# The two heads of a pair alternate block by block in the product of probabilities and values

## The chip, the cores and the metric

The kernel runs on one core of a Trainium2 chip. The metric is the device time of one execution in microseconds, as the median of several runs. The matrix engine (PE, TensorE) multiplies; its weight loads are recorded apart from its products (PEld). VectorE (DVE), ScalarE (ACT) and GpSimd (POOL) work element by element, and SyncE (SP) issues most transfers.

## The reference, cut to what matters

One decoder layer on a sequence of 512 tokens with width 1024: an adaptive RMS norm, a mixture of three causal dilated window attentions with 16 heads of 64 per group, an output projection, a gated convolutional feed-forward layer of width 2816, and a last norm. The change touches the attention alone:

```
def dilated_mixture_attention(h, w_in, w_out):
    qkv = (h @ w_in).reshape(B, S, 3, DSW_GROUPS, DSW_HEADS, DSW_HEAD_DIM)
    for g, (window, dilation) in enumerate(((128, 1), (512, 4), (2048, 16))):
        o, lse = dilated_window_attention(qkv[:, :, 0, g], qkv[:, :, 1, g], qkv[:, :, 2, g], window, dilation)
        ...
    weights = jax.nn.softmax(jnp.stack(lses, axis=0), axis=0)
    o = jnp.sum(weights[..., None] * jnp.stack(outs, axis=0), axis=0)
    return o.reshape(B, S, D_MODEL).astype(h.dtype) @ w_out
```

In each group a query attends to a band of keys. The probabilities, weighted by the mixture, times the values give `o`. That last product, `einsum('brnhqk,brnkhe->brnqhe', p / denom, v)`, is the one whose order is changed.

## The kernel before, in words

The 16 heads are worked in 8 pairs. A pair's heads stand side by side in 128 partitions: head 0 in partitions 0 to 63, head 1 in 64 to 127. `body` (line 716) runs nine passes: pass n projects q, k and v of pair n (nine strips of 1024 x 128 weights, each in two halves of 12 products, `half_strip`, lines 604 to 606) and, between these halves, does the attention of pair n - 1. The first pass only projects. The last, for the eighth pair, only attends, and fills the room between its steps with the first products of the output projection (`begin_out`, lines 684 to 686). Each engine has its program written out by hand, in the order of the half strips h = 0 to 17; semaphores join them.

Attention of a pair has four parts j = 0 to 3, each two tiles of 128 queries with up to two blocks of 128 keys. j 0 and 1 are the first group (bank 6), j 2 and 3 the two dilated groups (bank 7).

- `make_scores` (lines 621, 628): queries times keys, contraction over 64 partitions; the two heads already alternate there, into a bank each.
- VectorE adds the mask and takes the maximum (line 1202), ScalarE exponentiates (953), VectorE mixes and scales (1218), which it counts in `scaled`.
- `turn_probs` (line 657): the matrix engine transposes the scaled probabilities, head 0 into bank 4 and head 1 into bank 5. VectorE copies bank 4 into p_t (line 1192, semaphore `turn_taken0`), ScalarE bank 5 (line 923, `turn_taken1`). p_t has four slots; part j with head hd uses slot (2j + hd) mod 4.
- `weigh_values` (line 676): values (128 keys x 64 columns, the weights) times p_t (128 keys x 128 queries, moving), into `o_acc[side]`. Head 0's 64 columns go to PSUM partitions 0 to 63, head 1's to 64 to 127, of the same bank. j = 0 has three blocks per head, the others four.
- When the last part is through (`pv_done`), ScalarE copies bank 6 to o_a (966), VectorE adds bank 7 (1294), ScalarE rounds to oh (970), VectorE takes the rest as ol (1299), and `o_summed` lets the next pair's product begin.

The parts are placed by tables: transposes of part 0, 1, 2, 3 after half strip 12, 14, 15, 16, the product of part 0, 1, 2, 3 after half strip 14, 15, 16, 17, ahead of the transposes at the same place.

Of the kernel before, what the change touches and what calls it, by code (L numbers as in the profile page):

```python
# [25 lines left out]
P = 128  # L26
# [4 lines left out]
H, E = 16, 64  # L31
# [18 lines left out]
PT_RING = 4  # L50
# [25 lines left out]
def decoder_layer(nc, x, c, w_ada, b_ada, norm_mix, norm_ffn, attn_w_in, attn_w_out,  # L76
# [11 lines left out]
    with ctx:  # L88
# [3 lines left out]
        def sem(name):  # L92
            return ctx.enter_context(nc.semaphore(name))
# [28 lines left out]
        v_n = tensor(scope_a, "v_n", [P, 2, GROUPS, NT, P])  # L122
        v_t = tensor(scope_a, "v_t", [P, 2, T])
        probs = tensor(scope_a, "probs", [P, 2, 2, NT, HALF])
        p_t = tensor(scope_a, "p_t", [P, PT_RING, T])
# [46 lines left out]
        proj, score, turn, o_acc = banks[0:2], banks[2:4], banks[4:6], banks[6:8]  # L172
# [30 lines left out]
        turn_taken = [sem("turn_taken0"), sem("turn_taken1")]  # L203
        scored, masked, nmax_done, exp_done = sem("scored"), sem("masked"), sem("nmax_done"), sem("exp_done")
        swapped, mix_dve, mix_act = sem("swapped"), sem("mix_dve"), sem("mix_act")
        scaled, pv_done = sem("scaled"), sem("pv_done")
# [15 lines left out]
        def turns_before(n):  # L222

            return 0 if isinstance(n, int) and n == 0 else 6 * n - 4
# [7 lines left out]
        PV_AT = {14: 0, 15: 1, 16: 2, 17: 3}  # L232
# [307 lines left out]
        def _(pe):  # L540
# [4 lines left out]
            for t in range(KT):  # L545
                if t >= 4:
                    pe.wait_ge(start_taken, t - 3)
                for i in range(NT):
                    last = nc.tensor.transpose(banks[t % 4][:, P * i:P * (i + 1)], x_nat[:, i, P * t:P * (t + 1)], ident[:])
# [9 lines left out]
            for t in range(KT):  # L559
                pe.wait_ge(start_taken, KT + 2 + t - 3 if t >= 4 else KT - 3 + t)  # L560
                for i in range(NT):
                    last = nc.tensor.transpose(banks[t % 4][:, P * i:P * (i + 1)], xr_nat[:, i, P * t:P * (t + 1)], ident[:])
# [95 lines left out]
                                               probs[:, hd, j // 2, b, P * part:P * (part + 1)], ident[:])  # L658
                last.then_inc(turned[k], 1)

            def weigh_values(n, par, u, before):
                hd, j, k = u % 2, u // 2, u % 2
                e = slice(E * hd, E * (hd + 1))
                pe.wait_ge(turn_taken[k], turns_before(n) + before + j + 1)
                if u == 0:
                    pe.wait_ge(o_summed, n)
                side = j // 2
                blocks = p_blocks(j)
                for i, (b, part) in enumerate(blocks):
                    if side == 0:  # L670
                        values = v_n[:, par, 0, b - 1 + part, e]
                    else:
                        values = v_n[:, par, 1 + part, b, e]
                    first = i == 0 or blocks[i - 1][0] != b
                    final = i == len(blocks) - 1 or blocks[i + 1][0] != b
                    last = nc.tensor.matmul(o_acc[side][e, P * b:P * (b + 1)], values, p_t[:, u % PT_RING, P * i:P * (i + 1)],  # L676
                                            start=first, stop=final)
                last.then_inc(pv_done, 1)

            def out_tiles(o, tiles, tokens=slice(0, T)):  # L680
# [35 lines left out]
            def body(n, par, project, attend):  # L716
                before = 2 if project else 0
                filled = 0
                for h in range(2 * RING if is_first(n) else 0, HALVES):
                    s = h // 2  # L720
                    if project:
                        g = STRIPS * n + s
                        if h % 2 == 0:
                            pe.wait_ge(l_ready, g + 1)
                            if not (is_first(n) and s == RING):
                                pe.wait_ge(strip_taken, g - 1)
                        last = half_strip(qkv_bank(n, par, s), qkv_slot(n, s), h % 2, hh, hl)
                        if h % 2 == 1:
                            last.then_inc(strip_done, 1)
                        turn_v_at = TURN_V_FIRST if is_first(n) else TURN_V_AT  # L730
                        if h in turn_v_at:
                            turn_values(n, par, turn_v_at[h])
                        if h == (ADA_FIRST if is_first(n) else ADA_AT):
                            sum_ada(n)
                    if attend:
                        if h in SCORE_AT:
                            make_scores(n, 1 - par, SCORE_AT[h])
                        if h in PV_AT:
                            for u in (2 * PV_AT[h], 2 * PV_AT[h] + 1):
                                weigh_values(n, 1 - par, u, before)  # L740
                        if h in TURN_P_AT:
                            for u in (2 * TURN_P_AT[h], 2 * TURN_P_AT[h] + 1):
                                turn_probs(n, u, before)
                    if attend and not project and h in FILL_AT:
                        begin_out(fill_steps[filled:filled + FILL_AT[h]])
                        filled += FILL_AT[h]
# [21 lines left out]
            for hf in range(2):  # L768
                tokens = slice(HALF * hf, HALF * (hf + 1))
                for t in range(KT):  # L770
# [5 lines left out]
                    for j in range(2):  # L776
                        nc.tensor.matmul(banks[j][:, tokens], wl_first[:, j, t], fh[:, t, tokens], start=(t == 0), stop=False)
                        nc.tensor.matmul(banks[j][:, tokens], wh_first[:, j, t], fh[:, t, tokens], start=False, stop=False)
                        last = nc.tensor.matmul(banks[j][:, tokens], wh_first[:, j, t], fl[:, t, tokens],
                                                start=False, stop=(t == KT - 1))  # L780
# [49 lines left out]
            for o in range(KT):  # L830
                for k in (FT - 2, FT - 1):
# [3 lines left out]
                    last = nc.tensor.matmul(y_bank(o)[:], wh[:, slot, o], act_l[:, k], start=False, stop=(k == FT - 1))  # L835
                last.then_inc(y_done, 1)
                for m in BACK_AT.get(o, ()):

                    pe.wait_ge(x2_done, 4 if m < 4 else KT if m < 6 else KT + 1)
                    for q in range(4):  # L840
                        last = nc.tensor.transpose(y_bank(m)[:, P * q:P * (q + 1)],
                                                   xT[:, 4 * (m // 4) + q, P * (m % 4):P * (m % 4 + 1)], ident[:])
# [4 lines left out]
        def _(act):  # L847
# [77 lines left out]
            def body(n, par, project, attend):  # L925
                before = 2 if project else 0
                for h in range(HALVES):
                    s = h // 2
                    if project:
                        if split_at(n, h) is not None:  # L930
                            split_qkv(n, split_at(n, h))
                        if h % 2 == 1:
                            act.wait_ge(strip_done, STRIPS * n + s + 1)
                            kind, g = strip_of(s)

                            if is_first(n) and s == 2:
                                act.wait_ge(turned[0], 1)
                            dst = {"v": v_t[:, (par + g) % 2], "q": q_t[:, par, g], "k": k_t[:, par, g]}[kind]
                            src, dst = in_order(g, kind, qkv_bank(n, par, s)[:], dst)
                            nc.scalar.activation(dst, src, ACT.Copy).then_inc(strip_taken, 1)  # L940
                        if (TURN_V_FIRST if is_first(n) else TURN_V_AT).get(h) == 1:
                            take_turn(n, 0, v_n[:, par, 1].rearrange("p b e -> p (b e)"))
                    if attend and not project and h == 0:
                        split_out(split_h, 3, h_ready, wh)
                    if attend:
                        if h in SCORE_AT:
                            d = SCORE_AT[h]
                            act.wait_ge(nmax_done, 4 * (n - 1) + d + 1)
                            side = d // 2
                            for b in (2 * (d % 2), 2 * (d % 2) + 1):  # L950
                                for hd in range(2):
                                    tile = probs[:, hd, side, b, (P if d == 0 and b == 0 else 0):HALF]
                                    last = nc.scalar.activation(tile, tile, ACT.Exp, bias=nmax[:, side, b, hd:hd + 1],  # L953
                                                                scale=SCORE_SCALE, accum_out=stat[:, side, b, 1, hd:hd + 1])
                            last.then_inc(exp_done, 1)
                        if h == 8:
                            act.wait_ge(mix_dve, MIX_STEPS * (n - 1) + 3)
                            nc.scalar.activation(mix[:, 3:5], mix[:, 1:3], ACT.Exp, scale=SCORE_SCALE).then_inc(mix_act, 1)
                        if h in TURN_P_AT:
                            u = 2 * TURN_P_AT[h] + 1  # L960
                            take_turn(n, before + u // 2, p_t[:, u % PT_RING])
                    if is_last(n) and h == HALVES - 2:
                        split_out(split_h, 2, h_ready, wh)
                if attend:
                    act.wait_ge(pv_done, 8 * n)
                    nc.scalar.activation(o_a[:].rearrange("p (b j r) -> p b j r", b=NT, r=4),
                                         o_acc[0][:].rearrange("p (b r j) -> p b j r", b=NT, r=4),
                                         ACT.Copy).then_inc(oa_copied, 1)
                    act.wait_ge(o_summed, n + 1)
                    nc.scalar.activation(oh[:, bass.ds(n - 1, 1)].rearrange("p a n -> p (a n)"), o_sum[:],  # L970
                                         ACT.Copy).then_inc(oh_done, 1)
# [531 lines left out]
```

## Time and profile before

| | |
|---|---|
| median of 3 runs | 1021.26 us (1020.44 to 1022.64) |
| profiled execution, first to last instruction (its span) | 1017.7 us |
| matrix engine busy | 973.8 us, 96% |
| VectorE busy | 514.6 us, 51% |
| ScalarE busy | 403.3 us, 40% |
| product of probabilities and values (line 676), busy | 47.1 us |
| transposes of the probabilities (line 657), busy | 33.0 us |

Of the profiled execution the profile has the span alone; the runs are timed as a whole, and their median is 3.6 us more than the span. Busy time of a group is the time in which at least one of its records ran, so records that overlap aren't counted twice. The start of a matrix record is measured, its end modelled.

### The profile page before, as it was taken

To read this page: it belongs to the slowest core of one execution; us is meant where nothing else is said; L and a number is where in the kernel's file an instruction comes from. 1 tells how busy PE (TensorE), PEld (TensorE's weight loads), DVE (VectorE), ACT (ScalarE), POOL (GpSimd) and SP (SyncE) were. 2 spreads that over 40 slices of the span, in tenths; PEclk is the share of its full clock that TensorE was granted. 3 is DMA by queue.
4 is the path that set the end of the run, shared out by engine and by line. 5 is a ranking of instruction groups with operands and counts; after the bars stand their busy time and mean duration, and the time that the engine had idled before them with its cause. 6 is when DMAs were issued, how large, how long until landed. Compare 5 with 4: busy or idle time off the path is not lost.

```text
span 1017.7 us, 14215 instructions
## 1 busy us (share of the span) xinstructions
PE 973.8 (96%) x5008; PEld 784.4 (77%) x5008; DVE 514.6 (51%) x1115; ACT 403.3 (40%) x721; POOL 31.3 (3%) x43
## 2 busy tenths in 40 slices
PE   4589999999999999999999989999999999999996
PEld 3478787887877878878778779888888888888885
DVE  5863663655735646357365557644444444412214
ACT  7433443434435344353443534633333333321212
POOL 3500000000000000000000000100000000000000
PEclk9699999999999999999999999999999999999999
DMA  9746341432324314333232203333333323232212
GB/s 310 210 116 194 112 133 48 125 118 90 95 89 123 124 41 124 124 103 124 62 114 74 62 22 90 100 101 91 95 97 89 102 83 103 83 104 86 99 62 83
DMA packets 151533, 106.94 MB, mean 105 GB/s; under 512 B 3510, under 2 KB 138830, under 8 KB 151502
## 3 DMA queue, kind: packets, MB, share of 16 engines
q1 hardware_dynamic: 151296, 106.45, 34.4%
q8 instruction: 19, 0.31, 0.1%
q14 instruction: 12, 0.10, 0.0%
q10 hardware_dynamic: 206, 0.08, 0.0%
HBM read 104.42 MB, written 2.10 MB: 105 GB/s over the span
## 4 chain that ended last, share of the span: by engine, by line
PE 92%; DVE 5%; ACT 1%; issue 1%; DMA 1%; SPq 0%; DVEq 0%; POOL 0%; ACTq 0%
PE bank L604 13%; PE bank L606 13%; PE bank L605 13%; PE bank L797 8%; PE bank L798 8%; PE bank L799 8%; PE bank L676 4%; PE bank L822 4%; PE bank L821 4%; PE bank L823 4%; PE bank L657 3%; PE bank L628 2%; PE bank L621 1%; DVE acc L1093 1%; PE bank L684 1%; PE bank L686 1%
## 5 line engine op out<-in xcount | busy, mean ns | idle before, releaser
L1131 DVE TENSOR_TENSOR wl<-raw,wh 128x1024 fp32r<-128x1024 f32 x144 | 177.4, 1232 | 305.1 <-ACT wh L883 304.6
L883 ACT ACTIVATE wh<-raw 128x1024 fp32r<-128x1024 f32 x144 | 152.2, 1059 | 200.8 <-PE bank L799 112.9
L604 PE MATMUL bank<-hh,wl 128*128 128x512 f32 x552 | 227.0, 411 | 0.0
L606 PE MATMUL bank<-hl,wh 128*128 128x512 f32 x552 | 218.7, 396 | 0.0
L605 PE MATMUL bank<-hh,wh 128*128 128x512 f32 x552 | 218.3, 395 | 0.0
L799 PE MATMUL bank<-fl,wh 128*128 128x512 f32 x336 | 133.0, 396 | 0.0
L798 PE MATMUL bank<-fh,wh 128*128 128x512 f32 x336 | 133.0, 396 | 0.0
L797 PE MATMUL bank<-fh,wl 128*128 128x512 f32 x336 | 133.0, 396 | 0.0
L604 PEld LDWEIGHTS bank<-hh,wl 128*128 128x128 f32 x552 | 104.1, 189 | 27.8 <-issue 5.7
L606 PEld LDWEIGHTS bank<-hl,wh 128*128 128x128 f32 x552 | 103.9, 188 | 24.7
L605 PEld LDWEIGHTS bank<-hh,wh 128*128 128x128 f32 x552 | 104.1, 189 | 20.7
L953 ACT ACTIVATE probs<-probs,nmax 128x256 f32<-128x256 f32 (+1 forms) x128 | 61.9, 485 | 98.4 <-DVE nmax L1208 98.4
L797 PEld LDWEIGHTS bank<-fh,wl 128*128 128x128 f32 x336 | 63.2, 188 | 15.3
L799 PEld LDWEIGHTS bank<-fl,wh 128*128 128x128 f32 x336 | 63.2, 188 | 15.2
L798 PEld LDWEIGHTS bank<-fh,wh 128*128 128x128 f32 x336 | 63.2, 188 | 15.1
L822 PE MATMUL bank<-act_h,wh 128*128 (+1 forms) x160 | 63.4, 396 | 0.0
L823 PE MATMUL bank<-act_l,wh 128*128 (+1 forms) x160 | 63.4, 396 | 0.0
L821 PE MATMUL bank<-act_h,wl 128*128 (+1 forms) x160 | 63.3, 396 | 0.0
L1192 DVE COPY p_t<-bank 128x512 f32<-128x512 f32 x32 | 22.1, 690 | 61.7 <-PE bank L657 61.7
L923 ACT ACTIVATE p_t<-bank 128x512 f32<-128x512 f32 x32 | 19.1, 598 | 79.4 <-PE bank L657 79.4
L676 PEld LDWEIGHTS bank<-p_t,v_n 128*64 128x64 f32 x480 | 39.4, 136 | 12.0 <-issue 10.7
L676 PE MATMUL bank<-p_t,v_n 128*64 128x128 f32 x480 | 47.1, 279 | 0.3 <-DVE p_t L1192 0.3
(175 smaller groups left out, 1147.7 us busy)
## 6 DMA issues: line engine op xcount, KB each, us to landing
raw<-in_attn_w_in SPq DMA_DIRECT2D x72, 512.0 KB, 3.8
raw<-in_ffn_w_up SPq DMA_DIRECT2D x44, 512.0 KB, 3.8
ada_raw<-in_w_ada SPq DMA_DIRECT2D x16, 1024.0 KB, 5.7
raw<-in_ffn_w_down SPq DMA_DIRECT2D x22, 512.0 KB, 3.3
ada<-in_w_ada SPq DMA_DIRECT2D x16, 256.0 KB, 7.1
raw<-in_attn_w_out SPq DMA_DIRECT2D x8, 512.0 KB, 3.6
x_nat<-in_x SPq DMA_DIRECT2D x4, 512.0 KB, 5.2
x_nat<-in_w_ada SPq DMA_DIRECT2D x8, 256.0 KB, 6.3
```

Source lines behind the costliest of these rows:

```text
L604: nc.tensor.matmul(bank[:], wl[:, slot, t], xh[:, t], start=(t == 0), stop=False)
L605: nc.tensor.matmul(bank[:], wh[:, slot, t], xh[:, t], start=False, stop=False)
L606: last = nc.tensor.matmul(bank[:], wh[:, slot, t], xl[:, t], start=False, stop=(t == KT - 1))
L676: last = nc.tensor.matmul(o_acc[side][e, P * b:P * (b + 1)], values, p_t[:, u % PT_RING, P * i:P * (i + 1)], start=first, stop=final)
L797: nc.tensor.matmul(bank[:], wl[:, slot, t], fh[:, t], start=(t == 0), stop=False)
L798: nc.tensor.matmul(bank[:], wh[:, slot, t], fh[:, t], start=False, stop=False)
L799: last = nc.tensor.matmul(bank[:], wh[:, slot, t], fl[:, t], start=False, stop=(t == KT - 1))
L821: nc.tensor.matmul(y[:], wl[:, slot, o], xh, start=start, stop=False)
L822: nc.tensor.matmul(y[:], wh[:, slot, o], xh, start=False, stop=False)
L823: last = nc.tensor.matmul(y[:], wh[:, slot, o], xl, start=False, stop=False)
L883: nc.scalar.activation(dst, src, ACT.Copy).then_inc(done, 1)
L1131: nc.vector.tensor_tensor(dst, src, high.bitcast(F32), ALU.subtract).then_inc(done, 1)
```

## The change

In `weigh_values` the loop over the two heads moves inside the loop over blocks: where all blocks of head 0 stood ahead of all of head 1, block after block now comes for head 0 and then for head 1. The function is called once for a part and not once for a head, so it waits at its start for both heads' copies into p_t, and counts `pv_done` once a part (4 for a pair, where there were 8). No product is added, removed or resized, and the order within a head stays.

```diff
-            def weigh_values(n, par, u, before):
-                hd, j, k = u % 2, u // 2, u % 2
-                e = slice(E * hd, E * (hd + 1))
-                pe.wait_ge(turn_taken[k], turns_before(n) + before + j + 1)
-                if u == 0:
+            def weigh_values(n, par, j, before):
+
+                for k in range(2):
+                    pe.wait_ge(turn_taken[k], turns_before(n) + before + j + 1)
+                if j == 0:
                     pe.wait_ge(o_summed, n)
                 side = j // 2
                 blocks = p_blocks(j)
                 for i, (b, part) in enumerate(blocks):
-                    if side == 0:
-                        values = v_n[:, par, 0, b - 1 + part, e]
-                    else:
-                        values = v_n[:, par, 1 + part, b, e]
                     first = i == 0 or blocks[i - 1][0] != b
                     final = i == len(blocks) - 1 or blocks[i + 1][0] != b
-                    last = nc.tensor.matmul(o_acc[side][e, P * b:P * (b + 1)], values, p_t[:, u % PT_RING, P * i:P * (i + 1)],
-                                            start=first, stop=final)
+                    for hd in range(2):
+                        e = slice(E * hd, E * (hd + 1))
+                        if side == 0:
+                            values = v_n[:, par, 0, b - 1 + part, e]
+                        else:
+                            values = v_n[:, par, 1 + part, b, e]
+                        last = nc.tensor.matmul(o_acc[side][e, P * b:P * (b + 1)], values,
+                                                p_t[:, (2 * j + hd) % PT_RING, P * i:P * (i + 1)],
+                                                start=first, stop=final)
                 last.then_inc(pv_done, 1)
...
                         if h in PV_AT:
-                            for u in (2 * PV_AT[h], 2 * PV_AT[h] + 1):
-                                weigh_values(n, 1 - par, u, before)
+                            weigh_values(n, 1 - par, PV_AT[h], before)
...
-                    act.wait_ge(pv_done, 8 * n)
+                    act.wait_ge(pv_done, 4 * n)
```

The matrix engine in a pass that projects, at the product of part 2 (the fourth row from the top in the first fence is head 0, the sixth head 1), before:

```order
L605 MATMUL bank1<-hh,wh 128x512
L606 MATMUL bank1<-hl,wh 128x512
L664 REGISTER_ALU
L676 MATMUL bank7<-p_t,v_n 64x128 [waits turn_taken0]
L676 MATMUL bank7<-p_t,v_n 64x128 x3
L676 MATMUL bank7<-p_t,v_n 64x128 [waits turn_taken1]
L676 MATMUL bank7<-p_t,v_n 64x128 x3
L654 REGISTER_ALU
```

Four products of head 0 stood there, and then, behind a wait of their own, four of head 1. The same place now:

```order
L606 MATMUL bank1<-hl,wh 128x512
L664 REGISTER_ALU
L678 MATMUL bank7<-p_t,v_n 64x128 [waits turn_taken1,turn_taken0]
L678 MATMUL bank7<-p_t,v_n 64x128 x7
L654 REGISTER_ALU
```

Eight products stand behind both waits; every second one is head 1's. The matrix engine at the end of the last pass, transposes and product of part 3, before:

```order
L657 MATMUL bank4<-ident,probs 128x128 [waits turn_taken0,scaled]
L657 MATMUL bank4<-ident,probs 128x128 x3
L657 MATMUL bank5<-ident,probs 128x128 [waits turn_taken1,scaled]
L657 MATMUL bank5<-ident,probs 128x128 x3
L676 MATMUL bank7<-p_t,v_n 64x128 [waits turn_taken0]
L676 MATMUL bank7<-p_t,v_n 64x128 x3
L676 MATMUL bank7<-p_t,v_n 64x128 [waits turn_taken1]
L676 MATMUL bank7<-p_t,v_n 64x128 x3
```

And now:

```order
L657 MATMUL bank4<-ident,probs 128x128 [waits turn_taken0,scaled]
L657 MATMUL bank4<-ident,probs 128x128 x3
L657 MATMUL bank5<-ident,probs 128x128 [waits turn_taken1,scaled]
L657 MATMUL bank5<-ident,probs 128x128 x3
L678 MATMUL bank7<-p_t,v_n 64x128 [waits turn_taken1,turn_taken0]
L678 MATMUL bank7<-p_t,v_n 64x128 x7
```

Here nothing stands between the transposes and the product, and the wait for `turn_taken1` has moved from the fifth product to the first.

## Rows read from the trace of the kernel before

**Rows 1.** The page: busy time per engine; granted clock in 40 slices, in tenths.
```profile
PE 973.8 (96%) x5008; PEld 784.4 (77%) x5008; DVE 514.6 (51%) x1115; ACT 403.3 (40%) x721; POOL 31.3 (3%) x43
...
PEclk9699999999999999999999999999999999999999
```
**Rows 2.** Waits of PE, 78 to 604 us: us in total, times, longest.
```profile
PE bank L657 <- DVE probs L1218: 2.0, 1, 2.0
PE bank L621 <- DVE stat L1202: 0.8, 1, 0.8
PE bank L676 <- DVE p_t L1192: 0.3, 1, 0.3
```
**Rows 3.** Line 676: duration ns min/median/max, first and last start; who waits for it.
```profile
L676 PE MATMUL bank<-p_t,v_n x480: 272/273/325, 149.3 to 600.5; 128*64 128x128 f32 x160
...
  ACT o_a L966: 4.4, 8
```
**Rows 4.** Timeline of PE, 149 to 156 us: start, length, instructions.
```profile
148.96 0.40 PE L606 MATMUL bank<-hl,wh 128*128 128x512 f32 x1
149.29 1.15 PE L676 MATMUL bank<-p_t,v_n 128*64 128x128 f32 x12
...
154.18 1.58 PE L676 MATMUL bank<-p_t,v_n 128*64 128x128 f32 x16
```
**Rows 5.** Line 676: stretch, length, busy (records), PEld's; timelines at 154.96 and 155.30.
```profile
154.60:154.61 0.01, 0.01 (x3) 0.01 (x1) 1.00 0.00 0
154.94:154.95 0.01, 0.01 (x6) 0.01 (x3) 1.00 0.00 0
155.40:155.41 0.01, 0.01 (x3) 0.01 (x2) 1.00 0.00 0
...
154.67 0.54 PE L676 MATMUL bank<-p_t,v_n 128*64 128x128 f32 x5
...
155.05 0.71 PE L676 MATMUL bank<-p_t,v_n 128*64 128x128 f32 x5
```
**Rows 6.** Scores, line 628: one block, and its records in flight at 117.30.
```profile
116.68 1.16 PE L628 MATMUL bank<-k_t,q_t 64*128 64x128 f32 x16
...
117.30:117.31 0.01, 0.01 (x4) 0.01 (x4) 1.00 0.53 205
```
**Rows 7.** Timeline of ACT, 149 to 154 us.
```profile
151.49 0.60 ACT L923 ACTIVATE p_t<-bank 128x512 f32<-128x512 f32 x1 [2.95 <-PE bank L657]
```
**Rows 8.** Timeline of PE, ACT and DVE in the last pass, 592 to 600 us.
```profile
592.96 1.58 PE L676 MATMUL bank<-p_t,v_n 128*64 128x128 f32 x16
...
596.19 1.58 PE L676 MATMUL bank<-p_t,v_n 128*64 128x128 f32 x16
...
599.14 1.58 PE L676 MATMUL bank<-p_t,v_n 128*64 128x128 f32 x16 [0.35 <-DVE p_t L1192]
...
592.36 0.60 ACT L923 ACTIVATE p_t<-bank 128x512 f32<-128x512 f32 x1 [3.59 <-PE bank L657]
595.60 0.60 ACT L923 ACTIVATE p_t<-bank 128x512 f32<-128x512 f32 x1 [2.64 <-PE bank L657]
598.83 0.60 ACT L923 ACTIVATE p_t<-bank 128x512 f32<-128x512 f32 x1 [2.63 <-PE bank L657]
...
598.40 0.69 DVE L1192 COPY p_t<-bank 128x512 f32<-128x512 f32 x1 [2.54 <-PE bank L657]
```
**Rows 9.** Timeline of PE and ACT at the seam, 564 to 572 us.
```profile
564.49 1.58 PE L676 MATMUL bank<-p_t,v_n 128*64 128x128 f32 x16
566.00 0.93 PE L621 MATMUL bank<-k_t,q_t 64*128 64x128 f32 x8
...
569.98 1.13 PE L621 MATMUL bank<-k_t,q_t 64*128 64x256 f32 x8 [0.75 <-DVE stat L1202]
...
564.59 1.07 ACT L940 ACTIVATE k_t<-bank 128x512 f32<-128x512 f32 x1 [1.25 <-PE bank L606]
566.10 0.60 ACT L966 ACTIVATE o_a<-bank 128x512 f32<-128x512 f32 x1 [0.45 <-PE bank L676]
```

## The prediction

> **What bounds the kernel now.** I read the page first. The matrix engine is busy for 973.8 of 1017.7 us, with its clock granted in full (the 2.4 GHz level) from the third slice on, and VectorE and ScalarE for about half of the span or less [rows 1]. Then I read the waits of the matrix engine alone, from 78 us to 604 us, the stretch in which attention runs: three waits, 3.1 us in all, and none in the seven passes over a pair that also project [rows 2]. So up to about 566 us every nanosecond that comes off the matrix engine's own stream comes off the end, and the question is what the blocks of the product cost there.
>
> One block of `weigh_values` is 16 records on the matrix engine, 12 in the first block of a pair (each fp32 product is recorded as two: 480 records for 240 products [rows 3]). There are 32 blocks: 8 with 12 records and 24 with 16 (8 x 12 + 24 x 16 = 480). A 12-record block takes 1.15 us and a 16-record one 1.58 us, from the first start to the last end [rows 4]. The last record itself takes 0.27 us, so from first start to last start they take 0.88 and 1.31 us. Ahead of a block the engine's starts are 0.33 us apart (148.96 to 149.29 [rows 4]); the change leaves that as it is.
>
> **Inside a block.** Now the same block in its records. At the instant 154.60 three records are in flight, at 154.94 six, at 155.40 three again [rows 5]. Head 0 writes the lower 64 partitions of the bank and head 1 the upper 64, so they use different column halves of the array, and the middle stretch is both heads at once. The record that starts at 154.67 is still in flight at 154.96 [rows 5]; at over 0.29 us it is one of the long ones (325 ns at most, median 273 [rows 3]) that open a head. So head 1 begins at 154.67, 0.49 us after head 0 at 154.18, and runs to 155.76: 1.09 us, or 0.82 us from first to last start. Alone, its last five records take 0.71 us, a spacing of (0.71 - 0.27) / 4 = 0.11 us [rows 5]. A head's eight records are therefore 0.16 + 6 x 0.11 = 0.82 us, whether the other head runs beside it or not, and a block of today is a delay of 0.49 plus one head's 0.82 = 1.31 us. That is exactly the row. The block is long because head 1 is let in only when three records of head 0 are left; 0.49 us of each block have one half of the array at work, and the last 0.49 too.
>
> **What the change does to it.** The program has head 0, head 1, head 0, head 1, so head 1's first weights stand two records behind the start instead of eight. The place in this trace where heads already alternate like that is the scores, on the row halves (contraction 64): 16 records take 1.16 us, 0.89 from first to last start, with four in flight at 117.30 [rows 6]. Their weights are 64 rows by 128 columns [rows 6], the product's 128 by 64 [rows 3]. From both sides:
> - both heads fully side by side, 0.01 us apart: 0.82 + 0.01 = 0.83 us for 16 records, and 0.60 + 0.01 = 0.61 for 12 (two spacings of 0.11 fewer). Saved: 24 x 0.48 + 8 x 0.27 = 13.7 us.
> - as slow as the scores: 0.89 and, two spacings fewer, 0.67. Saved: 24 x 0.42 + 8 x 0.21 = 11.8 us.
> I take a value next to the first, 0.835 and 0.615, since head 1's pace beside head 0 is measured on the product itself, and the scores' slower start goes with their wider weights. That is 24 x 0.475 + 8 x 0.265 = 11.4 + 2.1 = 13.5 us.
>
> **The second wait.** The block now waits for both copies into p_t before its first record; head 1's used to be awaited 0.49 us later. In the passes that project a half strip of 12 products stands between the transposes and the block, and ScalarE's copy is 2.1 us early: it ends at 152.09, the block starts at 154.18 [rows 4, 7]. Nothing there. In the last pass, which only fills with a product or so, it counts. Both copies follow the transposes, so they shift with them, and only distances matter [rows 8]:
> - first block of that pass: three fills stand ahead of it, and the copies are long over. Nothing.
> - block at 592.96: ScalarE's copy ends at 592.96. From a copy's end to the engine's start 0.05 us pass (599.09 to 599.14). About 0.05 us late.
> - block at 596.19: ScalarE ends at 596.20. About 0.06 us late.
> - block at 599.14: it waits for VectorE already (599.09); ScalarE ends at 599.43, so it starts at 599.48: 0.34 us late.
> Sum 0.45 us. Queued behind each of these waits are the block itself and all of the engine's program; ScalarE and VectorE wait for it through `pv_done` and the next transposes.
>
> **The seam between the last two passes.** The block at 564.49 is followed by the scores, which need the k strip that ScalarE copies until 565.66 (564.59 + 1.07); they now stand at 566.00 [rows 9] and would be ready at 565.52, so they wait some 0.2 us. That costs nothing: after them come three fills and the second scores at 569.98, which already wait 0.75 us for VectorE. That wait hangs on the chain from the block's end over o_a, o_sum, oh and ol to the masks. o_a starts at 566.10, 0.45 us after ScalarE is free of the k strip, so the chain moves by 0.44 of the 0.475 us. Cost 0.04 us. The 2.0 us wait of the transposes for VectorE near 587 us [rows 2] is further along the same chain and moves with it.
>
> The one increment of `pv_done` per block instead of two moves nothing: ScalarE waits for the last alone, 4.4 us in eight passes [rows 3]. After 604 us the work is as before, only earlier.
>
> **Sum.** 13.5 - 0.45 - 0.04 = 13.0 us. The profiled execution's span goes from 1017.7 to 1004.7 us; the median of the runs lies 3.6 us above the span, for what lies around it, and goes from 1021.26 to **1008.3 us**.
>
> **Rivals.**
> *A. The column halves don't load beside each other when they alternate* (slower). If each record must wait for the other head's, 16 of them take 0.16 + 14 x 0.11 = 1.69 us instead of 1.31, and 12 take 1.25 instead of 0.88. That is 24 x 0.38 + 8 x 0.37 = 12.1 us more, and with the second wait 1033.8 us. It decides when the mean spacing in a block is over 1.31 / 15 = 0.087 us. Against it stands the six in flight at 154.94, at which both heads' weights were being loaded beside running products [rows 5]. For it: the two heads have now only crossed once per block, never switched at each product.
> The Trainium skill, "TensorE: Matmul & The Clock Gate", section "The mechanism" of Part 3, says that a weight load overlaps with running matmuls only where the row group differs, and that matmuls start and end in strict program order; both heads here have the same row group. By that rule rival A is what comes. Rows 5 speak against it: head 1 begins at 154.67 while three records of head 0 are still to start.
> *B. The change doesn't bring the heads closer.* The engine looks a few instructions ahead, and the two records of one product may have to be through before the other head's; then the block keeps its 1.31 us and only the waits are left: 1021.26 + 0.5 = 1021.7 us. The scores' rows speak against it, where two records of a product stand next to each other in the same way and four are in flight.
> *C. The last block of a pass gives its gain to a wait.* ScalarE's strip copy and the chain over o_a and ol could become what the next pass waits for, as at the last seam. Then 8 x 0.475 = 3.8 us are lost: 1012.1 us. For it: ScalarE is free for only 0.45 us ahead of o_a [rows 9]. Against it: in the passes that project, 12 products stand between the last block and the next scores, and the engine waits for nothing there.
>
> **How the numbers follow.** Forecast 0.82, A 0.06, B 0.06, C 0.06. About 0.2%, 2 us, is what a measurement tells from no change. The forecast and C are faster by more than that (0.88), B is the same (0.06), A slower (0.06). The bounds of the block's length give 1021.26 - 13.7 + 0.5 = 1008.1 to 1021.26 - 11.8 + 0.5 = 1010.0 us. With about 1.5 us on either side, which is less than a measurement tells from no change, the range is 1006.5 to 1011.5.
>
> **What would show it.** In the profile after, a 16-record block should last 1.10 us from first start to last end instead of 1.58, a 12-record block 0.88 instead of 1.15, with five or six records in flight from shortly after the start to shortly before the end. Blocks 1.5 us or longer show A or B. The waits of the matrix engine should gain two or three short ones for ScalarE's p_t in the last pass, under 0.4 us each, and one of 0.2 us for k_t. Any wait within a pass that projects would show C. A time above 1011.5 us would mean that one of these steps is wrong.

## The result and the profile after

| | before | changed |
|---|---|---|
| median of 4 runs | 1021.34 us (1020.44 to 1022.64) | 1009.38 us (1007.84 to 1010.49) |
| profiled execution, span | 1017.7 us | 1008.7 us |
| matrix engine busy | 973.8 us | 964.1 us |

The ratio is 0.9881, with a 95% interval of 0.9864 to 0.9898: 12.0 us faster where 13.0 were forecast. The profiled execution of the changed kernel took 1010.49 us, and was the slowest of its four.

The product's blocks in the timeline of the matrix engine of the changed kernel (start, length, instructions), which answer to [rows 4]; line 678 is the product, 657 the transposes:

```profile
151.73 0.88 PE L678 MATMUL bank<-p_t,v_n 128*64 128x128 f32 x12
...
156.03 0.40 PE L606 MATMUL bank<-hl,wh 128*128 128x512 f32 x1
156.36 1.09 PE L678 MATMUL bank<-p_t,v_n 128*64 128x128 f32 x16
```

A block of 16 records takes 1.09 us instead of 1.58, one of 12 takes 0.88 instead of 1.15, and the 0.33 us ahead of it are as they were. Less the last record's 0.27 us, that is 0.82 and 0.61 us. The records of line 678 in flight at three instants of that block (stretch, its length, busy time and records of PE, then of PEld, granted clock, transfers), which answer to [rows 5]:

```profile
156.60:156.61 0.01, 0.01 (x4) 0.01 (x2) 1.00 0.00 0
156.90:156.91 0.01, 0.01 (x6) 0.01 (x2) 1.00 0.00 0
157.10:157.11 0.01, 0.01 (x6) 0.01 (x3) 1.00 0.00 0
```

Four to six records are in flight over the block, where before six were only in the middle third. The duration of one did not move (the product's line of the profile gives minimum, median and maximum; [rows 3]):

```profile
L678 PE MATMUL bank<-p_t,v_n x480: 272/273/323, 151.7 to 591.5; 128*64 128x128 f32 x160
```

A block of both heads takes 0.82 us, what head 1 alone took inside the old block (0.82 us from 154.67 on), so the two heads cost each other nothing. Now the waits of the matrix engine from 78 to 592 us, against [rows 2] (the view lists idle stretches over 0.15 us):

```profile
PE bank L657 <- DVE probs L1220: 2.0, 1, 2.0
PE bank L678 <- ACT p_t L925: 0.8, 1, 0.8
PE bank L621 <- DVE stat L1204: 0.6, 1, 0.6
```

They are three again, all in the last pass: the last block's wait has grown from 0.3 to 0.8 us and is for ScalarE now. In the last pass, against [rows 8]:

```profile
582.16 0.88 PE L678 MATMUL bank<-p_t,v_n 128*64 128x128 f32 x12
...
584.84 1.09 PE L678 MATMUL bank<-p_t,v_n 128*64 128x128 f32 x16
...
587.74 1.09 PE L678 MATMUL bank<-p_t,v_n 128*64 128x128 f32 x16
...
590.63 1.09 PE L678 MATMUL bank<-p_t,v_n 128*64 128x128 f32 x16 [0.78 <-ACT p_t L925]
591.66 0.50 PE L687 MATMUL bank<-oh,wl 128*128 128x512 f32 x1
...
584.10 0.60 ACT L925 ACTIVATE p_t<-bank 128x512 f32<-128x512 f32 x1 [4.88 <-PE bank L657]
587.00 0.60 ACT L925 ACTIVATE p_t<-bank 128x512 f32<-128x512 f32 x1 [2.30 <-PE bank L657]
589.89 0.60 ACT L925 ACTIVATE p_t<-bank 128x512 f32<-128x512 f32 x1 [2.30 <-PE bank L657]
```

ScalarE's copies end at 584.70, 587.60 and 590.49, and the blocks start 0.14 us behind each. At the seam, against [rows 9]:

```profile
555.41 1.09 PE L678 MATMUL bank<-p_t,v_n 128*64 128x128 f32 x16
556.64 0.93 PE L621 MATMUL bank<-k_t,q_t 64*128 64x128 f32 x8
...
555.52 1.07 ACT L942 ACTIVATE k_t<-bank 128x512 f32<-128x512 f32 x1 [1.25 <-PE bank L606]
556.55 0.60 ACT L968 ACTIVATE o_a<-bank 128x512 f32<-128x512 f32 x1
```

The idle 0.45 us of ScalarE ahead of o_a are gone. The second scores start at 560.43, 5.02 us behind the block, where 5.49 us lay between them before.

**One thing more stands in this profile.** Behind the 2.04 us wait of the transposes the granted clock was half of full (1.2 GHz) for over 3 us. First the timeline of the matrix engine at that place, then a stretch of it, in the changed kernel:

```profile
577.58 1.01 PE L657 MATMUL bank<-ident,probs 128*128 128x128 f32 x6 [2.04 <-DVE probs L1220]
578.34 0.66 PE L687 MATMUL bank<-oh,wl 128*128 128x512 f32 x1
578.80 0.63 PE L688 MATMUL bank<-oh,wh 128*128 128x512 f32 x1
579.23 0.63 PE L689 MATMUL bank<-ol,wh 128*128 128x512 f32 x1
...
578.50:581.80 3.30, 3.30 (x10) 2.52 (x9) 3.23 (x12) 0.60 (x1) 0.00 (x0) 0.50 0.03 5
```

The products of the fills start 0.43 us apart there instead of 0.23. From the transposes to the first block of the pass 4.58 us go by (577.58 to 582.16), where it was 3.03 in the kernel before, whose rows are

```profile
587.13 1.01 PE L657 MATMUL bank<-ident,probs 128*128 128x128 f32 x6 [2.04 <-DVE probs L1218]
...
590.16 1.15 PE L676 MATMUL bank<-p_t,v_n 128*64 128x128 f32 x12
```

So 1.55 us are lost.

### The profile page after: what moved, and what is told of

It is laid out like the page before. It is cut to its first block, busy times and chain, and to the rows that moved or that the text cites. A ratio compares the mean times of both kernels' runs of the same rounds, so it can differ in the third digit from the quotient of the medians.

```text
span 1008.7 us, 14239 instructions
## 1 busy us (share of the span) xinstructions
PE 964.1 (96%) x5008; PEld 773.1 (77%) x5008; DVE 515.2 (51%) x1115; ACT 403.2 (40%) x721; POOL 31.1 (3%) x43
## 4 chain that ended last, share of the span: by engine, by line
PE 92%; DVE 4%; ACT 1%; issue 1%; DMA 1%; SPq 0%; DVEq 0%; POOL 0%; ACTq 0%
PE bank L604 13%; PE bank L606 13%; PE bank L605 13%; PE bank L801 8%; PE bank L799 8%; PE bank L800 8%; PE bank L823 4%; PE bank L825 4%; PE bank L824 4%; PE bank L678 3%; PE bank L657 3%; PE bank L628 2%; PE bank L621 1%; PE bank L687 1%; PE bank L688 1%; PE bank L689 1%
## 5 line engine op out<-in xcount | busy, mean ns | idle before, releaser
L1204 DVE CUSTOM_DVE_ANT_0 probs<-bank,mask 128x256 f32<-128x256 f32 (+1 forms) x128 | 44.4, 403 | 6.0 <-PE bank L628 6.0
L1240 DVE SCALAR_TENSOR_TENSOR acc<-ada_raw,cond,acc 128x512 f32<-128x512 f32 x56 | 41.9, 749 | 0.9 <-issue 0.3
```

## The experiments

Of every profile I take three lengths in us from the matrix engine's timeline: the start of the first block; the middle, from there to the first fill behind the last block (149.29 to 600.65 = 451.4 us in the kernel before); and the rest, from there to the end. The first lies before anything that the change touches. The one profile that isn't in the table is the first of "same half"; its numbers stand there.

| profile | first block starts | middle | rest | clock halved in the last pass |
|---|---|---|---|---|
| before | 149.3 | 451.4 | 417.0 | no |
| before, second | 151.7 | 451.4 | 417.1 | no |
| before, third | 151.3 | 451.4 | 417.0 | no |
| both waits first, old order | 149.9 | 452.0 | 417.0 | no |
| changed | 151.7 | 439.9 | 417.0 | yes |
| changed, second | 153.1 | 438.4 | 417.1 | no |
| changed, third | 152.5 | 439.9 | 417.0 | yes |
| wait at head 1 | 151.5 | 439.6 | 417.0 | yes |
| runs of two | 149.3 | 441.1 | 417.1 | yes |
| same half | 148.6 | 464.3 | 417.0 | no |
| fills ahead, old order | 148.7 | 450.4 | 417.0 | no |
| fills ahead | 151.5 | 437.5 | 417.0 | no |
| fills ahead, wait at head 1 | 149.2 | 437.3 | 417.1 | no |

**Both waits first, old order.** Is any part of the gain the waits'?

```diff
 def weigh_values(n, par, u, before):      # the kernel before
...
-    pe.wait_ge(turn_taken[k], turns_before(n) + before + j + 1)
+    if hd == 0:
+        for w in range(2):
+            pe.wait_ge(turn_taken[w], turns_before(n) + before + j + 1)
```

> The order of before (all of head 0, then all of head 1), with both waits for the p_t copies ahead of head 0. Theory: the waits change nothing in the passes that project, and cost 0.7 to 0.8 us in the last pass, as the trace of the changed kernel has it (0.05, 0.14 and 0.15 us and 0.43 us on top of the old wait); a block of 16 records stays at 1.58 us. Time 1022 us, no difference that can be measured. Rival: both waits together also let head 1's weights in earlier, and part of the gain comes from them: blocks shorter than 1.5 us and a time below 1018.

Measured: 1022.04 us (10 runs) against 1021.37, ratio 1.001 (0.9999 to 1.0022). The middle is 0.6 us longer. A block ahead of which both copies were long done keeps its length, and in the last pass one takes 1.55 us instead of 1.58:

```profile
593.70 1.55 PE L678 MATMUL bank<-p_t,v_n 128*64 128x128 f32 x16
597.05 1.55 PE L678 MATMUL bank<-p_t,v_n 128*64 128x128 f32 x16
600.41 1.55 PE L678 MATMUL bank<-p_t,v_n 128*64 128x128 f32 x16 [0.78 <-ACT p_t L925]
```

The 0.8 us wait is there without any alternation. It follows that the waits give nothing and cost 0.6 us, and that the wait in front of head 1's first product isn't what held head 1 back in the old block: without it the block is still 1.58 us. The gain is the order's.

**Same half.** Is it the column halves that let the heads run side by side? Both heads write the lower 64 partitions.

```diff
-    last = nc.tensor.matmul(o_acc[side][e, P * b:P * (b + 1)], values,
+    last = nc.tensor.matmul(o_acc[side][0:E, P * b:P * (b + 1)], values,
...
-                            start=first, stop=final)
+                            start=True, stop=True)
```

> The changed kernel, but both heads write PSUM partitions 0 to 63, so both use the same column half of the array, and every product stands alone (no accumulation). Head 1's share goes over head 0's, and what the output holds is not the attention. Theory: the halves are what lets the heads run side by side; without them 16 records follow each other at 0.11 us, 0.16 + 14 x 0.11 = 1.69 us from first to last start (12 records 1.25 us), 24 x 0.87 + 8 x 0.65 = 26 us over the changed kernel, 1035 us. Rival: the gain comes from the alternation of p_t slots and accumulators; the block stays at 0.82 us and the time at 1009.

> The kernel in which both heads write PSUM partitions 0 to 63 and no product accumulates (its output is not the attention), once more, since the first profile of it came from an execution in which the matrix engine ran at half speed throughout. Theory: 16 records take 1.69 us from first to last start, 12 records 1.25 us, and the time is 1033 us as in its one undisturbed run. Rival: 1.31 us or less in a block, with the time lost elsewhere.

Measured the second time: 1032.51 us (4 runs) against 1020.05, ratio 1.0125 (1.0106 to 1.0143). The first time one run took 1033.26 us and the profiled one 1972.43, with 0.44 to 0.45 us between the starts of the projection's products where it is 0.23; nothing is read from it. The timeline of the second and an instant of it:

```profile
148.63 1.52 PE L678 MATMUL bank<-p_t,v_n 128*64 128x128 f32 x12
...
153.90 1.96 PE L678 MATMUL bank<-p_t,v_n 128*64 128x128 f32 x16
...
154.90:154.91 0.01, 0.01 (x2) 0.01 (x1) 1.00 0.00 0
```

1.96 - 0.27 = 1.69 us and 1.52 - 0.27 = 1.25 us, with two or three in flight: the one-by-one pace of rival A. The middle is 25.9 us longer than the changed kernel's without a clock fall (464.3 - 438.4). This is the same instruction order as in the changed kernel, so the order alone gives nothing; the place of the result is what decides. The edit also ends the accumulation (`start=True, stop=True`), and no run changes one without the other. But the scores' products have these two flags as well, and their heads, on the two row halves, do run side by side (four in flight, 0.89 us for 16 records [rows 6]), so the flags by themselves don't keep heads apart. The run also shows what the old order was worth: its heads overlapped by 0.38 us in a block (1.69 - 1.31).

**Runs of two.** How far must the heads be apart in the program?

```diff
-    for i, (b, part) in enumerate(blocks):
-        for hd in range(2):
+    order = [(i, hd) for lo in (0, 2) for hd in range(2) for i in range(lo, min(lo + 2, len(blocks)))]
+    for i, hd in order:
...
```

> Two blocks of head 0, two of head 1, two of head 0, two of head 1 (runs of four records instead of two). Theory: head 1 is let in when three records of head 0 are left ahead of it, so with runs of four records it starts right behind the first, and the block lasts 0.82 us from first to last start as in the changed kernel: 1009 to 1010 us. Rival: only a change of head at every product lets them run side by side; then the block lies between 0.82 and 1.31 us, 1.0 to 1.1, and the time at 1013 to 1016 us.

Measured: 1010.39 us (4 runs) against 1021.37, ratio 0.9909 (0.989 to 0.9928).

```profile
149.28 0.88 PE L679 MATMUL bank<-p_t,v_n 128*64 128x128 f32 x12
153.92 1.15 PE L679 MATMUL bank<-p_t,v_n 128*64 128x128 f32 x16
```

A block takes 1.15 - 0.27 = 0.88 us, neither the 0.82 of the theory nor the 1.0 to 1.1 of the rival, but close to the theory. Head 1 starts 0.01 us behind head 0's first record (153.93 and 153.92), while three of the four records in front of it are still to start, as in the old block, where it had to wait for five of eight to start. In the records one head's fifth, the first of its second run, is a long one of 0.32 us like those that open a block, and that head comes out 0.05 us late; that its weights weren't in ahead of time is my reading and not shown. Head 1 need not stand right behind each product of head 0; four records of the other head in front of it cost 0.05 us, eight cost 0.49 us [rows 5]. No run has a number between four and eight, so where the step lies is open.

**Wait at head 1.** Is the price of the second wait in its place?

```diff
-    for k in range(2):
-        pe.wait_ge(turn_taken[k], turns_before(n) + before + j + 1)
+    pe.wait_ge(turn_taken[0], turns_before(n) + before + j + 1)
...
+            if i == 0 and hd == 1:
+                pe.wait_ge(turn_taken[1], turns_before(n) + before + j + 1)
```

> The changed kernel with the wait for head 1's copy in front of head 1's first product. Theory: the three late blocks of the last pass end with head 1, whose copy by ScalarE comes last, so at most the 0.1 us that a wait of its own costs over one that is carried by the product comes back in each: 0.1 to 0.3 us in all, nothing in the time (1009.4 give or take the spread of single runs). Rival: the whole 0.7 us of the second wait comes back, the last block starts at the copy by VectorE and ends 0.4 us earlier against its transposes.

Measured: 1009.94 us in its one run.

```profile
584.47 1.15 PE L679 MATMUL bank<-p_t,v_n 128*64 128x128 f32 x16
587.27 1.15 PE L679 MATMUL bank<-p_t,v_n 128*64 128x128 f32 x16
589.79 1.43 PE L679 MATMUL bank<-p_t,v_n 128*64 128x128 f32 x16 [0.35 <-DVE p_t L1195]
```

The last block starts at VectorE's copy again and waits inside: 1.43 us long instead of 1.09. The middle is 0.3 us shorter than that of the changed kernel, both with the clock fall, as the theory has it. Only head 0's first product runs ahead of the inner wait; head 1 starts 0.05 us behind ScalarE's copy (590.08 to 590.13), so the 0.14 us above aren't a trait of ScalarE. What is lost at the last block is lost to ScalarE's copy, wherever the wait stands; the old order hid it behind 0.49 us of head 0.

**The changed kernel again, and the kernel before twice more.** Does the clock fall belong to the change?

> The changed kernel once more. Theory: its blocks take 0.82 and 0.60 us again, and where the time lies above the 1008.3 us forecast, the clock is halved for 3.4 us behind the 2.0 us wait for VectorE in the last pass, as in three of three profiles of the alternating kernels so far and none of two with the old order; it costs 1.5 us. Rival: the fall is chance and not tied to that wait; then this profile may have none, and its span is 1.5 us shorter from there on.

> The kernel before once more, for its profile. Theory: whether the clock is halved for 3.4 us behind the 2.0 us wait in the last pass doesn't hang on the order of the heads, since a second profile of the changed kernel had none. The profiles with that wait so far: 3 of 5 with alternating heads or runs, 0 of 2 with the old order. So it may come here too, and then costs 1.5 us; the first block starts anywhere from 148.6 to 153.1 us, as in the profiles so far. Rival: the old order never has it.

> The same, a third profile of the kernel before. Theory: the fall of the clock in the last pass comes in some executions of either order; blocks at 1.31 and 0.87 us always. Rival: never with the old order, and a first block at 148.7 to 149.9 us each time, while the alternating kernels start theirs later.

> A third profile of the changed kernel. Theory: 438.3 to 438.4 us from the first block's start to the first fill behind the last block where the clock stays, 439.9 where it falls; start of the first block anywhere from 148.6 to 153.1 us. Rival: another length, so that something beside the clock differs from execution to execution.

Measured: the changed kernel 1009.09 us (4 runs) against 1021.19, ratio 0.9873 (0.9842 to 0.9904), then 1011.18 once; the kernel before 1021.91 and 1021.46. In the second profile of the changed kernel the same wait of 2.04 us is followed by a clock that stays:

```profile
578.91 1.01 PE L657 MATMUL bank<-ident,probs 128*128 128x128 f32 x6 [2.04 <-DVE probs L1220]
...
580.22 0.40 PE L689 MATMUL bank<-ol,wh 128*128 128x512 f32 x1
580.45 0.40 PE L687 MATMUL bank<-oh,wl 128*128 128x512 f32 x1
...
581.94 0.88 PE L678 MATMUL bank<-p_t,v_n 128*64 128x128 f32 x12
```

Here 3.03 us lie between transposes and block (578.91 to 581.94), as before the change, and the middle is 438.4 us. In the third it falls again, at 439.9. My expectation for the second profile had "tied to that wait" as theory and "chance" as rival; neither is whole. In the last pass the clock falls only behind that wait, but not each time: in 4 of 6 profiles with alternating heads or runs and the long wait (same half is one of the six), in 0 of 4 with the old order. For the kernel before I had expected it in some execution too, and its three profiles have none. Between the profiles of one kernel the lengths of the middle leave nothing else to explain. The changed order isn't enough for the fall, since the second profile has the same order and the same wait without it. Whether it makes it likelier, or 4 of 6 and 0 of 4 are chance, stays open; when the wait comes within an execution differs from profile to profile (it ends at 576.2 to 597.2 us), and no run holds that fixed. The late start of the first profile, by contrast, is no part of the change: the kernel before starts its first block at up to 151.7 us, too.

**Fills ahead.** Two of the 28 fills go from behind the transposes into the 2.0 us wait ahead of them.

```diff
-        FILL_AT = {1: 3, 3: 3, 5: 3, 7: 10, 12: 3, 14: 1, 15: 1, 17: 4}
+        FILL_AT = {1: 3, 3: 3, 5: 3, 7: 12, 12: 1, 14: 1, 15: 1, 17: 4}
```

> The changed kernel with two of the three fills of half strip 12 in the last pass moved ahead of the transposes, into the 2.0 us wait for VectorE (12 instead of 10 at h = 7, 1 instead of 3 at h = 12). Theory: the wait shrinks from 2.0 to 0.6 us, two fills of 0.7 us leave the path, and with the short wait the clock isn't halved: 1.4 + 1.5 us faster than the changed kernel, 1006.5 us, minus up to 0.3 us for a first block that now waits for the copies. Rival: the clock falls all the same, and only 1.4 us or less are gained, 1008 us.

> The kernel before with the same two fills moved. Theory: no halved clock to save here, so 1.4 us minus up to 0.3 us, 1020.1 us. Rival: the order of the fills is worth as much as in the changed kernel, 3 us, 1018.4 us.

> Both: the two fills moved, and the wait for head 1's copy in front of head 1's first product. Theory: 0.3 us better than the run with the fills alone in the trace, 1006.2 us, the fastest of all. Rival: with less work between transposes and blocks the copies are what is waited for, and the late wait gives nothing more.

Measured, all against 1021.19 us: with the changed order 1006.95 us (6 runs), ratio 0.9859 (0.9834 to 0.9884); with the old order 1019.46 (12 runs), 0.9986 (0.9971 to 1.0); with the wait at head 1 as well 1005.66 (5 runs, 1005.33 to 1006.71), 0.9846 (0.9822 to 0.987). The last in the matrix engine's timeline:

```profile
575.00 1.01 PE L657 MATMUL bank<-ident,probs 128*128 128x128 f32 x6 [0.64 <-DVE probs L1221]
...
577.11 0.88 PE L679 MATMUL bank<-p_t,v_n 128*64 128x128 f32 x12 [0.39 <-DVE p_t L1195]
```

The wait is 0.64 us instead of 2.04, no profile of the three has a clock fall, and the first block now waits 0.39 us for its copy. The middle is 0.9 us shorter than without (438.4 to 437.5 with the new order, 451.4 to 450.4 with the old): the 1.4 us of two fills less the 0.5 us by which the first block is late, where I had allowed 0.3. With a clock fall avoided it is 2.4. The wait at head 1 gives 0.2 us more, 437.3, not 0.3. This last version has the lowest median of all; its interval overlaps that of the changed kernel (0.9842 to 0.9904), but its longest run, 1006.71, is below the shortest of the changed kernel's four beside it, 1007.16, and the middles agree (437.3 against 438.4 at best).

## Why the prediction was right

- *What bounds.* The matrix engine alone, up to the last pass. In a pass that projects, the time between two passes' first blocks went from 66.61 us (149.29 to 215.89) to 64.89 (151.73 to 216.62): 1.72, which is 3 x 0.49 + 0.27 with nothing given back. Rival C is out.
- *The length of a block.* Forecast 0.835 and 0.615 us, measured 0.82 and 0.60 to 0.61, the better bound: 24 x 0.486 + 8 x 0.269 = 13.8 us (the records' starts to the nanosecond) where 13.5 were written. The scores' 0.89 was the wrong neighbour; what head 1 did beside head 0 in the middle of the old block was the right one, and the halves were the reason (same half).
- *The second wait.* 0.45 us forecast, 0.15 + 0.15 + 0.43 = 0.73 us measured: the places were right and each was 0.1 us short, since I took the 0.05 us that lie between VectorE's copy and a block with one wait, and the blocks with both waits start 0.14 us behind ScalarE's.
- *The seam.* 0.2 us of wait ahead of the scores, hidden, as forecast; the chain moved by 0.47 of 0.486 us where 0.44 were written.
- *Sum.* The three corrections cancel, which is luck: the middle went from 451.4 to 438.4 us, 13.0, in the profile without a clock fall, and to 439.9 in the two with one.
- *What was not in it.* The clock fall behind the 2.0 us wait, 1.5 us in two of three profiles of the changed kernel; I had written that this wait "moves with" the chain and counted it at nothing. It is of the size of the 1 us between the forecast of 1008.3 and the measured 1009.4, and the two kernels with fills ahead, whose profiles have no fall, are 12.5 us apart (1019.46 and 1006.95); but the runs without a profile don't tell whether they had it, and the start of the first block spreads by more than 1 us, so this is not shown. And the 3.6 us between span and median compared two executions: each run is 1.8 us over its own span (1010.49 and 1008.7), so the profiled execution before took about 1019.5, a short one (the start of the first block spreads over 4.4 us in the 13 profiles of the table). That moves both kernels alike and leaves the 13.0 us as they are.
- *Rivals A and B.* B, a block that keeps its 1.31 us, is out with 0.82 us. A's pace is real, 0.11 us a record, but needs both heads in one half. The rule of the Trainium skill that spoke for it ("TensorE: Matmul & The Clock Gate", "The mechanism": overlap of a weight load only where the row group differs, matmuls in strict program order) does not hold here: two heads in the same rows and different columns are 0.82 us for 16 records, and in the old block head 1's first record started at 154.67, ahead of head 0's last three (the one that counts up `pv_done` for head 0 started at 155.00).

## What to carry to other kernels

Where small products go to different halves of the array, look at the records in flight inside a block and not at its busy time: the engine counted as 96% busy while half of it stood idle for 1 us in each block. Alternate the halves in the program, product by product or in short runs. A wait that is moved ahead of the block costs what used to run in its shade, 0.15 to 0.43 us a block here. Loose work belongs where the engine waits in any case: two fills moved into the 2.0 us wait gave 0.9 us.

## What the runs showed of the hardware

- Two column halves of the array take 128 x 64 fp32 weights and 128 moving columns each at 0.11 us a record, with no loss to each other; in one half the same 32-bit products follow at 0.11 us in all.
- The engine starts a product of the other half ahead of earlier ones of this half: past three records, in the old block and with runs of two. With eight in front, head 1 starts 0.49 us late.
- A wait of 2.04 us was followed by over 3 us at 1.2 GHz in some executions and not in others of the same kernel (4 of 10 profiles with that wait), and cost 1.5 us in the two of the changed kernel that had it (439.9 against 438.4); behind 0.64 us it was not seen in three profiles.
- A block behind both waits started 0.14 us after ScalarE's copy where that came last (590.49 to 590.63), but 0.05 us after VectorE's where that did (fills ahead: 579.42 to 579.47). Behind a single wait the start followed 0.05 us after either engine (599.09 to 599.14 for VectorE, 590.08 to 590.13 for ScalarE with the wait at head 1). What makes the 0.14 isn't shown.
